# Two-layer hybrid backbone: partial products of the modulations folded by accumulating transfers instead of summed by TensorE

## What is computed

```python
sc = jax.nn.silu(c)                    # latent stream
scc = jax.nn.silu(c_ctx)[None, :]      # context stream
for l in range(DEPTH):                 # DEPTH = 2, N_MOD = 9
    m  = jnp.split((sc  @ w_ada[l] + b_ada[l])[:, None, :], N_MOD, axis=-1)
    mc = jnp.split((scc @ w_ada[l] + b_ada[l])[:, None, :], N_MOD, axis=-1)
    h = h + 0.5 * m[2] * swiglu(modulate(rmsnorm(h, g1[l]), m[0], m[1]), w_in1[l], w_out1[l])
    ...   # mixing (RG-LRU + spatial gating) with m[3], m[4], m[5]
    ...   # second swiglu with m[6], m[7], m[8]; the same for hc with mc
```

## Time and profile before

| | |
|---|---|
| median of 3 runs | 1578.04 us (1577.11 to 1578.14) |
| span of the profiled execution | 1575.5 us |
| TensorE busy | 1561.2 us, 99% of the span |
| VectorE busy | 1001.6 us, 64% |
| ScalarE busy | 631.0 us, 40% |
| GpSimd busy | 82.5 us, 5% |
| transfers | 249.95 MB, mean 159 GB/s, all issued by SyncE |

### The profile page before, as it was taken

How to read it: one execution, slowest core, us unless ns; L and a number is a source line. 1 busy time by engine, 2 the same in 40 slices (tenths; PEclk the granted TensorE clock), 3 DMA queues, 4 the chain that set the end, 5 groups by cost and what they waited for, 6 DMA issues and landing times.

```text
span 1575.5 us, 22302 instructions
## 1 busy us (share of the span) xinstructions
PE 1561.2 (99%) x9052; PEld 1338.1 (85%) x9052; DVE 1001.6 (64%) x1243; ACT 631.0 (40%) x856; POOL 82.5 (5%) x100
## 2 busy tenths in 40 slices
PE   8999999999999999999999999999999999999998
PEld 6888888888988888888888898888888897999998
DVE  5776773783967577777364267777445358975554
ACT  4433322332784343323222243333232249764553
POOL 0000000011100200000000100000000111000001
PEclk9999999999999999999999999999999999999999
DMA  9565553653322355565353336556354323456563
GB/s 365 201 197 179 186 162 119 208 192 94 115 75 79 94 166 193 176 201 173 107 196 99 107 121 201 193 183 195 100 173 148 107 91 108 147 188 197 190 203 117
DMA packets 71786, 249.95 MB, mean 159 GB/s; under 512 B 11664, under 2 KB 11920, under 8 KB 70672
## 3 DMA queue, kind: packets, MB, share of 16 engines
q1 hardware_dynamic: 71696, 248.70, 48.1%
HBM read 247.62 MB, written 1.05 MB: 158 GB/s over the span
## 4 chain that ended last, share of the span: by engine, by line
PE 96%; DVE 2%; ACT 1%; issue 0%; POOL 0%; POOLq 0%; DVEq 0%; ACTq 0%
PE bank L437 85%; PE bank L574 2%; PE bank L580 2%; PE bank L576 2%; PE bank L452 1%; PE bank L475 1%; PE bank L747 1%; PE bank L720 1%; PE bank L718 1%; PE bank L719 1%; PE bank L749 0%; PE bank L468 0%; DVE w_lo L1174 0%; PE bank L529 0%; PE bank L460 0%
## 5 line engine op out<-in xcount | busy, mean ns | idle before, releaser
L877 ACT ACTIVATE w_hi<-raw 128x1024 fp32r<-128x1024 f32 x317 | 335.9, 1060 | 807.0 <-PE bank L437 792.8
L1174 DVE TENSOR_TENSOR w_lo<-raw,w_hi 128x1024 fp32r<-128x1024 f32 x317 | 387.7, 1225 | 371.9 <-ACT w_hi L877 371.6
L437 PE MATMUL bank<-z_hi,w_hi 128*128 128x512 f32 (+1 forms) x1480 | 535.9, 362 | 2.4 <-DVE w_lo L1174 1.9
L437 PE MATMUL bank<-z_lo,w_hi 128*128 128x512 f32 (+1 forms) x1480 | 532.1, 360 | 0.0
L437 PE MATMUL bank<-z_hi,w_lo 128*128 128x512 f32 (+1 forms) x1480 | 531.9, 359 | 0.0
L437 PEld LDWEIGHTS bank<-z_hi,w_hi 128*128 128x128 f32 x1480 | 278.0, 188 | 49.7 <-DVE w_lo L1174 3.2
L437 PEld LDWEIGHTS bank<-z_hi,w_lo 128*128 128x128 f32 x1480 | 278.0, 188 | 42.6
L437 PEld LDWEIGHTS bank<-z_lo,w_hi 128*128 128x128 f32 x1480 | 278.1, 188 | 42.6 <-issue 1.0
L437 PE MATMUL bank<-h_hi,w_hi 128*128 128x512 f32 (+1 forms) x770 | 266.5, 346 | 0.0
L437 PE MATMUL bank<-h_lo,w_hi 128*128 128x512 f32 (+1 forms) x770 | 265.7, 345 | 0.0
L437 PE MATMUL bank<-h_hi,w_lo 128*128 128x512 f32 (+1 forms) x770 | 265.6, 345 | 0.0
(11 more groups left out here) (185 smaller groups left out, 1234.3 us busy)
## 6 DMA issues: line engine op xcount, KB each, us to landing
raw<-weights SPq DMA_DIRECT2D x320, 512.0 KB, 4.1
ada_raw<-ada_w SPq DMA_DIRECT2D x128, 512.0 KB, 4.2
ada_head<-head_w SPq DMA_DIRECT2D x8, 1024.0 KB, 18.5
res<-x_t SPq DMA_DIRECT2D x4, 512.0 KB, 4.8
ada_raw<-gate_w SPq DMA_DIRECT2D x4, 256.0 KB, 5.3
ws<-sgu_w SPq DMA_DIRECT2D x2, 256.0 KB, 4.0
bs<-sgu_b SPq DMA_DIRECT2D x2, 256.0 KB, 4.2
out<-final SPq DMA_DIRECT2D x2, 256.0 KB, 3.0
```

The lines of the kernel that those rows point to most:

```text
L437: m = pe.matmul(bank[:, to], w, x[:, k, at], start=start and i == 0, stop=stop and i == 2, skip_group_check=True)
L877: act.activation(w_hi[:, r, :], raw[:, r, :], ACT.Copy).then_inc(hi_ready, 1)
L1174: dve.tensor_tensor(w_lo[:, r, :], raw[:, r, :], w_hi[:, r, :].bitcast(F32), ALU.subtract).then_inc(lo_ready, 1)
```

## The change

The sum over partitions leaves TensorE. For each modulation GpSimd issues six accumulating transfers within SBUF (`fold`): two that add the upper 64 partitions of the one half of the columns to the lower 64, and the lower to the upper for the other half; then, when these have landed, four that add 32 partitions to 32, so that each group of 32 partitions holds a quarter of the 2x1024 columns, summed down to 32 rows. VectorE turns the four quarters by 32x32 blocks and sums each block's rows (`ada_turn`: four transposes of 32x512, one reduction of 128x512). ScalarE copies the result to `mods` in 16 small instructions, one slot later. `sel` and PE's `ring_sum` go, with PE's wait for `mods_ready` in the mixing part.

VectorE's turn of modulation m stands before its work on slot first+8m+10, at most slot 37 (`TURN_LAG`, `TURN_BY`). GpSimd's folds stand in its order before the `prep` calls of the same stage; in a down stage inside the sums of squares, after the first and the fourth (`FOLD_AT`). `UP_MODS` and `DOWN_MODS` become up 4, down 2, up 3, down 2, up 3, down 2.

```diff
...
 assert sorted(ADA_ORDER) == [(l, m) for l in range(DEPTH) for m in range(NMOD)][2:]
-UP_MODS = {(0, 0): 4, (0, 1): 4, (1, 0): 4, (1, 1): 0}
-DOWN_MODS = {(0, 0): 2, (0, 1): 1, (1, 0): 1, (1, 1): 0}
+UP_MODS = {(0, 0): 4, (0, 1): 3, (1, 0): 3, (1, 1): 0}
+DOWN_MODS = {(0, 0): 2, (0, 1): 2, (1, 0): 2, (1, 1): 0}
 RING_FROM = 4
+TURN_LAG = 10
+TURN_BY = UP_SLOTS - 7
+FOLD_AT = (1, 4)
...
         bd = ada_raw.rearrange("p r (b c) -> p (r b) c", c=P)
-        sel = sb("sel", [P, 2, 32])
         ada_turned = sb("ada_turned", [P, 2 * KD, 32])
+        ada_sums = sb("ada_sums", [P, 2, 2 * KD])
         scr = sb("scr", [P, 3, T])
...
         hi_ready, lo_ready, slot_done = sem("hi_ready"), sem("lo_ready"), sem("slot_done")
-        acc_first, acc_done, acc_read = sem("acc_first"), sem("acc_done"), sem("acc_read")
-        turned, mods_ready = sem("turned"), sem("mods_ready")
+        acc_first, acc_done = sem("acc_first"), sem("acc_done")
+        halves_folded, quarters_folded = sem("halves_folded"), sem("quarters_folded")
+        turned, summed, mods_ready = sem("turned"), sem("summed"), sem("mods_ready")
         head_in = [sem(f"head_in{i}") for i in range(KD)]
...
-        def ring_full(at, t):
-
-            m, k = divmod(t - at["first"], KD)
-            if k or not 1 <= m <= at["mods"] or (m % 2 and m < at["mods"]):
-                return ()
-            return range(at["mod"] + (m - 1) // 2 * 2, at["mod"] + m)
+        def turn_of(at, t):
+
+            for m in range(at["mods"]):
+                if t == min(at["first"] + KD * m + TURN_LAG, TURN_BY):
+                    return at["mod"] + m
+            return None
...
             return mod * 2 * (KD - 1) + (k - 1) * 2 + st + 1
+
+        def quarter(g):
+
+            first = (g % 2) * D + (g // 2) * 512
+            return slice(first, first + 512)
...
                 return m
-
-            def ring_sum(at, t):
-
-                full = ring_full(at, t)
-                if not full:
-                    return
-                pe.wait_ge(mods_ready, MODS0 + full[0])
-                pe.wait_ge(acc_done, acc_count(full[-1], KD - 1, 1))
-                for i, mod in enumerate(full):
-                    w = acc_of(at, mod).rearrange("p s (b j i) -> p s b j i", b=KD, j=4)
-                    for st in range(2):
-                        for j in range(4):
-                            m = pe.matmul(p_ada[32 * j:32 * j + 32, i * 256:i * 256 + 256], sel[:, st, :], w[:, st, :, j, :],
-                                          start=(st == 0), stop=(st == 1), tile_position=(0, 32 * j))
-                m.then_inc(acc_read, len(full))
...
                         slot(t // 4, t % 4)
-                        ring_sum(at, t)
                 else:
...
                         m.then_inc(slot_done, 1)
-                        if len(ss) == 2:
-                            ring_sum(at, q)
...
                             pe.wait_ge(bd_zero, l + 1)
-                            pe.wait_ge(mods_ready, MODS0 + AT["norm", n]["mod"])
                         if u == 1 and sets == 2:
...
                     if mod >= 2:
-                        act.wait_ge(acc_read, mod - 1)
+                        act.wait_ge(turned, 4 * (mod - 1))
                     for st in range(2):
...
                                        scale=c_cols[:, 0, st:st + 1]).then_inc(acc_first, 1)
+                mod = turn_of(at, t - 1)
+                if mod is not None:
+                    act.wait_ge(summed, mod + 1)
+                    src = ada_sums[:, mod % 2, :].rearrange("p (b j) -> p b j", j=4)
+                    for g in range(4):
+                        rows = slice(mod * KD + 4 * (g // 2), mod * KD + 4 * (g // 2) + 4)
+                        for j in range(4):
+                            act.activation(mods[32 * j:32 * j + 32, rows, g % 2], src[32 * g:32 * g + 32, :, j],
+                                           ACT.Copy).then_inc(mods_ready, 1)
...
-            def ada_turn(mod, n):
-
-                dve.wait_ge(mods_ready, MODS0 + mod)
-                dve.transpose(ada_turned[:, 0:n * KD, :].rearrange("p b r -> p (b r)"), p_ada[:, 0:n * 256]).then_inc(turned, n)
-                dve.wait_ge(turned, mod + n)
-                dve.tensor_copy(mods[:, mod * KD:(mod + n) * KD, :], ada_turned[:, 0:n * KD, 0:2]).then_inc(mods_ready, n)
+            def ada_turn(at, mod):
+
+                acc = acc_of(at, mod).rearrange("p s n -> p (s n)")
+                dve.wait_ge(quarters_folded, 64 * (mod + 1))
+                for g in range(4):
+                    own = slice(32 * g, 32 * g + 32)
+                    dve.transpose(ada_turned[own, :, :].rearrange("p b r -> p (b r)"), acc[own, quarter(g)]).then_inc(turned, 1)
+                dve.wait_ge(turned, 4 * (mod + 1))
+                if mod >= 2:
+                    dve.wait_ge(mods_ready, MODS0 + 16 * (mod - 1))
+                dve.tensor_reduce(ada_sums[:, mod % 2, :], ada_turned[:], AX_X, ALU.add).then_inc(summed, 1)
...
-                full = ring_full(at, t - 1)
-                if full:
-                    dve.wait_ge(acc_read, full[-1] + 1)
-                    ada_turn(full[0], len(full))
+                mod = turn_of(at, t)
+                if mod is not None:
+                    ada_turn(at, mod)
...
                 at = [ADA_ORDER.index((l, 3 * i + j)) for j in range(2)]
-                pool.wait_ge(mods_ready, MODS0 + max(at) + 1)
+                pool.wait_ge(mods_ready, MODS0 + 16 * (max(at) + 1))
                 a, b = at[0] * KD, at[1] * KD
...
                 at = ADA_ORDER.index((l, 3 * i + 2))
-                pool.wait_ge(mods_ready, MODS0 + at + 1)
+                pool.wait_ge(mods_ready, MODS0 + 16 * (at + 1))
                 a = at * KD
...
+            def fold(at, mod):
+
+                acc = acc_of(at, mod)
+                low, high = slice(0, 64), slice(64, P)
+                pool.wait_ge(acc_done, acc_count(mod, KD - 1, 1))
+                pool.dma_start(acc[low, :, 0:512], acc[high, :, 0:512], accum_op=ALU.add).then_inc(halves_folded, 16)
+                pool.dma_start(acc[high, :, 512:D], acc[low, :, 512:D], accum_op=ALU.add).then_inc(halves_folded, 16)
+                pool.wait_ge(halves_folded, 32 * (mod + 1))
+                acc = acc.rearrange("p s n -> p (s n)")
+                for g in range(4):
+                    own, other = slice(32 * g, 32 * g + 32), slice(32 * (g ^ 1), 32 * (g ^ 1) + 32)
+                    pool.dma_start(acc[own, quarter(g)], acc[other, quarter(g)], accum_op=ALU.add).then_inc(quarters_folded, 16)
+
             def norm(n):
                 w = dft(n)
+                down = AT[(n - 1) // 3, "down", (n - 1) % 3 // 2] if n % 3 != 2 and n else None
                 for d in range(1, 1 + pool_sums(n) - pool_sums(n - 1) if n not in (0, 3 * DEPTH - 1) else 1):
...
                     pool.tensor_tensor(scr[:, 2, 0:w], scr[:, 2, 0:w], scr[:, d % 2, 0:w], ALU.add).then_inc(sqsum_ready, 1)
+                    if down is not None and d in FOLD_AT[:down["mods"]]:
+                        fold(down, down["mod"] + FOLD_AT.index(d))
                 if n == 3 * DEPTH:
...
             pool.memset(ones[:], 1.0)
-            pool.memset(sel[:], 0.0)
             link(pool.memset(ident[:], 0.0))
-            for s in range(2):
-                pool.memset(sel[:, s, s:s + 1], 1.0)
             pool.affine_select(out=ident[:], in_=ident[:], compare_op=ALU.not_equal, fill=1.0, base=0,
...
             for l in range(DEPTH):
+                up = AT[l, "up", 0]
+                for m in range(3):
+                    fold(up, up["mod"] + m)
                 prep_gate(l, 0)
                 prep_norm(l, 1)
+                for m in range(3, up["mods"]):
+                    fold(up, up["mod"] + m)
                 norm(3 * l + 1)
...
                 norm(3 * l + 2)
+                up = AT[l, "up", 1]
+                for m in range(up["mods"]):
+                    fold(up, up["mod"] + m)
                 prep_gate(l, 2)
...
                     prep_norm(1, 0)
```

## The result

The changed kernel takes 1582.22 us, the median of 20 runs (1578.68 to 1586.35). The kernel before, beside it, takes 1577.52 (20 runs). The ratio is 1.0029, 95% interval 1.0022 to 1.0037: **slower by 0.3%**, where 1562.8 us and 1% faster were forecast. The profiled execution has a span of 1580.1 us, 4.6 more than before.

The account below looks back on a forecast made before the run. TensorE's chain (96% of the chain that ended last) was taken as the bound: span 1575.5 - 15.0 for the sums - 0.2 for the head = 1560.3, plus 2.5 to the median = 1562.8 us; range 1561.3 to 1568.

Parts of the forecast that it names:

- What goes: TensorE's sums over partitions: seven pairs at 1.86 us and two singles at 1.00, 15.0 us off its chain.
- What comes, VectorE and ScalarE: VectorE's turn, 3.5 us a modulation, fits its idle time; ScalarE's 16 copies, 3.2 us, just fit; 0 us.
- The fold: GpSimd's six transfers a modulation: 12 us taken, between 4.9 if each step's overlap and 18.2 if none do; 0 us.
- The fold may take 22.9, 23.7 and 18.3 us before TensorE waits: Free fold time: first up stage's third modulation 22.9, down stage about 23.7, first up stage's fourth modulation 18.3.
- VectorE's own 14.5 us: First up stage, third modulation: from last additions' end to VectorE reaching the turn, 14.5 us in which the fold costs nothing.
- 0 us each: Moved modulations, SyncE's later transfers, GpSimd's later prep calls and sums of squares, 12 MB more traffic: no cost.
- The end: Program's end: left unchanged inside the span; 2.5 us from profiled span to median of runs carried over.
- GpSimd holding VectorE: GpSimd's transfers stalling VectorE's additions: put at 0, with an end of 6.2 us a modulation, still within idle 12.4.
- The counts and SyncE's queue: One modulation moved from up to down in two places, SyncE issuing the same transfers later: 0 us.
- partly uncovered: Rival: fold takes 23 to 23.8 us, or 18 to 20 with VectorE held; 1572 us, half 1568; chance 0.10.
- The slower outcome: Rival: fold becomes the bound at VectorE's wait in up stages, from 23.9 us on; 1629 us at 27; chance 0.08.

Follow-up runs that it names:

- the padding: Changed kernel plus 128 bytes a partition behind ada_sums, so tiles behind it stand at their old offsets; 1585.51 us, median of 12, ratio 1.0012.
- the kernel with the counts alone: Kernel before with modulation counts 4, 2, 3, 2, 3, 2, sums still by TensorE; 1578.08 us, median of 12, ratio 1.0005.
- the three causes: Changed kernel with 128 bytes behind ada_sums, the turn one slot later and the last two output rows on VectorE; 1561.56 us, ratio 0.9887.
- the last rows on VectorE: Changed kernel with the last two output rows multiplied by VectorE and not GpSimd; 1579.03 us, median of 12, ratio 0.9988.
- one transfer: Kernel before with one plain 4 KB transfer within SBUF issued by GpSimd at its start; 1585.11 us, median of 12, ratio 1.0008.
- 128 and 256 bytes of padding: Kernel before with that many bytes a partition added behind ada_turned; 128: 1588.79 us, median of 9, ratio 1.0046; 256: 1585.68 us in one run.
- the smaller set: Changed kernel with 32 floats behind ada_sums, TURN_LAG 11 and the last output rows on VectorE; 1561.56 us, median of 6, ratio 0.9887.

## Why the prediction was wrong

**What goes: right in kind, 15.0 us where 17.2 were measured.** I took 1.86 us a pair from the earlier trace rows. The same matmuls come 2.09 us sooner for each pair, since the intervals on either side of the sum, 0.32 and 0.33 us in place of 0.227, go as well: 7 x 2.09, two singles at 1.2, and 0.3 us in the mixing part, where TensorE's wait for `mods_ready` went.

**What comes, VectorE and ScalarE: right.** Transposes 0.70 us each and the reduction 0.686, against 0.71 and 0.685 forecast; ScalarE's copies 0.205 against 0.20:

```profile
L976 ACT ACTIVATE mods<-ada_sums 32x4 f32<-32x4 f32 x256 | 52.5, 205 | 10.9 <-DVE ada_sums L1185 5.1
L1185 DVE TENSOR_REDUCE ada_sums<-ada_turned 128x16 f32<-128x512 f32 x16 | 11.0, 686 | 0.6
```

**The fold: 13.7 to 19.2 us where I took 12.** From the last addition's end to the first transpose, which waits for the last landing each time, the sixteen folds take 16.8 us in the mean, and three of them (19.2, 18.8 and 18.5 us, all in up stages) lie over my upper bound of 18.2. The longest is the second of the first up stage:

```profile
135.58 2.48 DVE L1353 SCALAR_TENSOR_TENSOR up_acc<-ada_raw,c_cols,up_acc 128x1024 f32<-128x1024 f32 x2
...
157.25 1.43 DVE L1181 STREAM_TRANSPOSE ada_turned<-up_acc 32x512 f32<-32x512 f32 x2 [5.68 <-DMA up_acc<-up_acc]
```

The four that matter below take 16.8 us (third modulation of the first up stage), 13.7 (its fourth), 17.7 and 16.7 (first down stage). A fold is two steps, one behind the other: in the one of 16.7 us the two transfers of 256 KB have landed 9.6 us after the last addition, and the four of 64 KB 6.8 us after GpSimd begins to issue them. My price of a landed transfer came from SyncE's loads and stores; those of GpSimd take 7.1 us (256 KB) and 5.0 to 5.5 (64 KB) in the median. The Trainium skill (Collectives: The Full Stack, section "The bandwidth ceiling: the fold count and why AG ≠ RS ≠ AR") states the half rate of an add for ReduceScatter between cores. With my bounds doubled by it, 9.8 to 36.4 us as an estimate, all sixteen lie inside; but no run here compares an accumulating with a plain transfer of one size, so the factor stays unshown.

**"The fold may take 22.9, 23.7 and 18.3 us before TensorE waits": the step that failed first.** It failed in two ways. The first: the down stage's 23.7 was taken over "by the same count" and not counted. The last row of such a stage takes slots 21, 22 and 23 together and waits at its start for the `w_lo` of all three, while the turn stands at slot 18, ahead of two of them. From the rows above: TensorE is ready at 378.79 - 2.05 = 376.74, from the transposes' start to the end of that `w_lo` it is 2.94 + 0.60 + 2.35 us, and the additions end at 356.12. That leaves 14.7 us, and the fold took 16.7. The second: I counted one modulation at a time, against the times of before. A fold longer than VectorE's own 14.5 us makes the next additions late, and TensorE, relieved of the sums, comes sooner. For the fourth modulation both together took the free 18.3 us down to about 13.4 (additions end at 228.86, TensorE is ready at 246.53, turn and product take 4.3), and the fold took 13.7. In the up stages' first three modulations the 22.9 us held: folds up to 19.2 us cost TensorE nothing. With the padding in, the turn one slot later removes all of these waits. The step was too cheap as well: I priced a late fold at one us for each us, and the wait of 2.05 us cost 3.8, with the clock that fell behind it.

**"0 us each" for what moves: wrong by the addresses.** I read the change of `sel` and `ada_sums` in the diff as two memsets and a reduction, and not as 128 bytes by which `h_hi`, `h_lo`, `y_hi` and `y_lo` move. That cost 11.5 us, the largest part of what came on top. But the parts do not simply add: with the padding alone the slower matmuls went and the waits grew by 7.8 us. No row of before could price the move. But the diff names it, and the rivals held no case for it.

**The end: not looked at.** I carried over the 2.5 us from the span to the median of the runs, left the end inside the span as it was, and charged GpSimd's transfers only where they are issued. The longer drain added 4.5 us.

**GpSimd holding VectorE: right at 0.** Additions of the up stages take 1279 ns in the mean after and 1280 before, so the 6.2 us of that end did not come. The rule of the Trainium skill that I set beside it (SBUF — State Buffer, section "Who interferes with whom") agrees with these 1279 and 1280 ns.

**The counts and SyncE's queue: right at 0,** by the kernel with the counts alone.

Of the rivals, "partly uncovered" is the nearest: TensorE did wait for folds, 6.0 us in sum with the half clock behind one wait, but in two down stages and the first up stage's fourth modulation, not 0.6 us in each of sixteen. The slower outcome that I had described, a fold over 23.9 us in the up stages, is not what happened: the longest took 19.2. With the three causes away the program takes 1561.56 us, and the forecast was 1562.8; that nearness is partly luck, since 2.2 us more are saved than I counted.

## What to carry to other kernels

When a tile is removed or added, work out which tiles behind it move and by how much modulo 256 bytes, and look at the interval of matmuls that read them: the move of 128 bytes cost 11.5 us here, and one line of padding took that back, once the waits that it had hidden were gone too. Count the slack of a new wait at each kind of stage by itself, at the last row or slot above all, with the waits ahead of it in place and against the times that the change leaves. Add to a wait of TensorE what its clock may lose behind it. And look at how the program ends when an engine is given its first transfers.

## What the runs showed of the hardware that I had not expected

- The address of the moving operand changes a matmul's interval: 227 ns at the old offset and at +256 bytes, 233 in the mean (229 to 238) at +128, 229 in the mean at +64, all with 512 columns; in the last down stage (256 columns) 113, 118 and 120 ns at 0, +128 and +64, in executions that have the `z` operands there at 113. Granted clock (1.00) and instructions are the same.
- GpSimd's drain at the program's end lasts 1.36 us and 0.082 more for each transfer it has issued: 1.46 with 1, 5.30 with 48, 9.23 with 96. Where it begins some 15 us before the other engines' end it lasts 8.70 with 96.
- A wait of TensorE can cost more than its length. Behind the wait of 2.05 us in the changed kernel the granted clock was 0.51 from 379.7 to 383.1 us, and 256-column matmuls started every 213 ns in place of 120. In the trace with the padding alone the same came with waits of 3.55 and 2.83 us, in the one with the last rows on VectorE with a wait of 2.18 us. But its waits of 1.88 and 2.20 us had no such stretch, and neither had those of 1.48 us and less behind a fold.
- The looped last stage runs at 113 or at 118 ns a matmul, `z` operands too. By its times the kernel before does both; the traces that have its code at 118 are those with one transfer and with 128 and 256 bytes of padding. Rows of the kernel before and of the same kernel with 256 bytes of padding, in its last down stage:

```profile
1539.77 0.28 PE L437 MATMUL bank<-h_hi,w_hi 128*128 128x256 f32 x1
1539.88 0.28 PE L437 MATMUL bank<-h_lo,w_hi 128*128 128x256 f32 x1
1540.00 0.28 PE L437 MATMUL bank<-h_hi,w_lo 128*128 128x256 f32 x1
1540.11 0.28 PE L437 MATMUL bank<-h_hi,w_hi 128*128 128x256 f32 x1
```

```profile
1539.81 0.28 PE L438 MATMUL bank<-h_hi,w_lo 128*128 128x256 f32 x1
1539.93 0.28 PE L438 MATMUL bank<-h_hi,w_hi 128*128 128x256 f32 x1
1540.05 0.28 PE L438 MATMUL bank<-h_lo,w_hi 128*128 128x256 f32 x1
1540.16 0.28 PE L438 MATMUL bank<-h_hi,w_lo 128*128 128x256 f32 x1
```

What chooses the rate stays open; the granted clock is 1.00 in both, and no run here was made to tell.
- The head of the program starts TensorE's steady work up to 2.6 us later in some executions (2.6 in the profiled one of the smaller set, 1.9 with 256 bytes of padding, both against the profiled one of before), which bounds how finely single runs compare. In both the granted clock is at its lower level for some us within the head (0.51 from 22.2 to 25.6 us in the smaller set), and it is 1.00 there in the profiled execution of before.
